# Key pages of a paged stick-breaking decode: one 1024-column product and one segmented sum in place of eight multiply-and-sum instructions

## The chip, the cores and the metric

The kernel runs on one NeuronCore of a Trainium2 chip, in one launch. The metric is the device time of one execution in microseconds (us), and the median of several runs is given. One further execution was taken with the hardware profiler; all rows below are from it.

The engines have these names: PE is TensorE (matrix products; its weight loads are PEld), DVE is VectorE, ACT is ScalarE, POOL is GpSimd, SP is SyncE, which here only issues transfers. They run side by side and wait for each other on semaphores.

## What is computed

The reference is one step of a two-layer decoder over a prompt of 512 rows and 8 sample rows, with width 2048, all in float32. Layer 0 has gated linear attention and retention; layer 1 has stick-breaking attention with 8 heads of 128 and a chunked spatial-gating MLP. Each layer ends in an output projection and a residual. The change lies in layer 1, in the attention of the samples over their past of 2048 positions, held in pages of 128 positions x 8 heads x 128 (512 KB each, 16 pages per sample):

```python
k_past = cache_k[i][page_table].reshape(dec_b, n_past, HC, DC)
z = (jnp.einsum('bqhd,bshd->bhqs', q, k) * (q.shape[-1] ** -0.5)
     + offset.astype(jnp.float32)[None, :, None, None])
log_beta = jax.nn.log_sigmoid(z)
log_rest = jnp.where(mask, jax.nn.log_sigmoid(-z), 0.0)
between = lax.cumsum(log_rest, axis=3, reverse=True) - log_rest
weight = jnp.where(mask, jnp.exp(log_beta + between), 0.0)
```

For a sample there is one query per head, so the scores of a page are 128 x 8 numbers: for each position and head a sum over 128 products of key and query.

## The kernel before

**The products.** All large projections are made in units. A unit is 8 chunks of 128 rows of a weight tile of 128 columns; each weight is split into a high and a low part, and three products (high x high, high x low, low x high) are summed, on two halves of 260 columns: 48 products per unit, all recorded at L548 (the helper `mm`). ACT makes the high part (`hi`, L973, recorded at L971), DVE the low part (`lo`, L1341, recorded at L1349). Both write one of two buffers, so the splits of unit u+2 are made when PE has finished unit u (semaphore `pe_tile`). SP loads the weights into five slots of `raw`.

**The order around the change.** Layer 1 has a first stage `l1a` (16 tiles: queries and the MLP's v) and a second `l1b` with one pass for each of 8 heads, 10 units each. The other work of a stage is written as a Python generator per engine (`l1a_mix`, `mix1`) and is woven between the units by `walk`: after a unit each engine goes one step further in its generator. On DVE `walk` (L1365) first makes the low split of the unit two ahead, and then takes the step. `l1b` runs head 0, then a hardware loop of three bodies with heads 1 and 2, 3 and 4, 5 and 6, then head 7.

**A pass of `l1b`** (`mix1` on DVE, L1818; on PE, L845; on ACT, L1220) does the prompt's attention for head i and the sample attention for sample i, both beside the 10 units. The steps on DVE that matter here:

- step 6 (L1882 to L1885) scales the prompt's scores `z` and takes their absolute value; ACT then runs exp and ln over `za`;
- step 7: `keys(7)`, then L1889 and the masks (L1787) finish `za` ("rest"), which PE's product "between" (L896 to L903) waits for;
- step 8: `keys(8)`, then the argument of a GELU (L1721 to L1723);
- step 9: L1897 on the product's result, `keys(9)`, then masks again ("weight"), which PE's output product (L909 to L915) waits for;
- step 10: L1903 to L1906, then `keys(10)`, the last of the pass.

**The key pages.** `keys(at)` stands at steps 1, 3, 4, 5, 7, 8, 9 and 10 (`KEYS_AT`, L69) and works on two pages of the next sample, i + 1; so head passes 0 to 6 have key pages and pass 7 has none. Sample 0's sixteen pages are worked on in steps 23 to 35 of `l1a` (`KEYS0_AT`, L68), one per step at first, two per step in the last three. `key_page` (L1725) waits for the page's transfer and makes eight `tensor_tensor_reduce` instructions, one per head, each of which multiplies 128 columns of the page by 128 columns of `qb` (the query row, the same on all partitions) in place and sums them into one column of scores. In the trace such an instruction is two records, CUSTOM_DVE_ANT_0 and the read of its accumulator, both at L1733. The last one raises `k_free`.

The pages have five slots: two for keys (`key_slot`, p % 2) and three for values. POOL fetches key pages (`key_page`, L1976, issue at L1982): page p waits for `k_free` of page p - 2. SP fetches value pages (L458) between weight loads, and PE works on them.

**Fences.** DVE instructions that read what the one before wrote are separated by a semaphore: `step(...)` (class `Chain`, L321) lets the instruction raise `dve_step` and waits for it. In a hardware loop the value waited for is worked out from the loop's index and the number of steps per body, which is why `step.body(n, 0, 24)` gets that number.

Of the kernel before, what the change touches and what calls it, by code (L numbers as in the profile page):

```python
# [9 lines left out]
ALU = mybir.AluOpType  # L10
ACT = mybir.ActivationFunctionType

P = 128
# [12 lines left out]
HC = 8  # L26
# [97 lines left out]
def build(nc, a, o, cst):  # L124
    ctx = ExitStack()
    with ctx:
# [5 lines left out]
        def s(name):  # L132
            if name not in sems:
                sems[name] = ctx.enter_context(nc.semaphore(name))
            return sems[name]
# [22 lines left out]
        def region(n):  # L158
            at = used[0]
            used[0] += n  # L160
            assert used[0] <= 16600, used[0]
            return arena[:, at:at + n]
# [50 lines left out]
        pages = region(5 * 1024).rearrange("p (n d) -> p n d", n=5)  # L213
        srow = mrow[:, 128:512]
        brow = mrow
        qb = region(1024)
# [92 lines left out]
        def key_slot(p):  # L309

            return p % 2
# [1025 lines left out]
        def _(dve):  # L1337
            step = Chain(dve, "dve_step")
            tt, ts_, stt, copy = dve.tensor_tensor, dve.tensor_scalar, dve.scalar_tensor_tensor, dve.tensor_copy
# [385 lines left out]
            def key_page(b, p, to):  # L1725

                if p == 0:
                    dve.wait_ge(s("qb"), b * 16 + 16)
                slot = key_slot(p)
                dve.wait_ge(s(f"page{slot}"), b * 128 + 16 * (p // 2 + 1))  # L1730
                for h in range(HC):
                    kpage = pages[:, slot, P * h:P * h + P]
                    last = dve.tensor_tensor_reduce(kpage, kpage, qb[:, P * h:P * h + P], 1.0, 0.0,  # L1733
                                                    ALU.mult, ALU.add, to[:, 8 * p + h:8 * p + h + 1])
                last.then_inc(s("k_free"), 1)

            def key_pages(b, k, to):

                for p in (2 * k, 2 * k + 1):
                    key_page(b, p, to)  # L1740
# [21 lines left out]
            def l1a_mix():  # L1762
                for n in range(L1A_STEPS):
                    for r in range(4):
                        if n == Q_SUM[r] + 1:
                            dve.wait_ge(s("q_rs"), r + 1)
                            for t in range(2):
                                last = stt(wide[:, 2 * r + t, :], G[r % 2 * 2 + t], cols[:, C_QN:C_QN + 1], tmp[t],
                                           ALU.mult, ALU.mult)
                            step(last)  # L1770
                        value_gate(r, n - V_AT[r])
                    if n == Q_SUM[3] + 1:
                        copy(qcol.rearrange("p (b h) -> p h b", b=NB), wide[:, 0:HC, T:N]).then_inc(s("q_col"), 1)
                    for p in range(NPAGE):
                        if n == KEYS0_AT[p]:
                            key_page(0, p, zs[0])
                    yield
# [132 lines left out]
            def l1b(i, odd, last=False):  # L1910
                mix = mix1(i, odd, last)
                walk("l1b", i, L1B_ORDER, None, mix=mix)
                finish(mix)
# [1 line left out]
            l1b(0, 0)  # L1915
            step.straight()
            with dve.Fori(0, 3) as n:
                step.body(n, 0, 24)
                l1b(n * 2 + 1, 1)
                l1b(n * 2 + 2, 0)  # L1920
            step.end(3, 24)
            l1b(7, 1, True)
            rows_kept(8)
            dve.wait_ge(s("pe_tile"), tile_no("out1", 0, 0))
# [229 lines left out]
```

## Time and profile before

| | |
|---|---|
| median of 3 runs | 2234.89 us (2234.24 to 2239.43) |
| the profiled execution | 2237.85 us, its span 2236.3 us |
| mean granted clock of PE | 0.974 of full speed |
| instructions | 45304 |
| PE busy | 2116.0 us (95%) |
| DVE busy | 1156.1 us (52%) |
| ACT busy | 605.5 us (27%) |
| POOL busy | 200.5 us (9%) |
| `l1a` and `l1b`, up to the last output product | about 1140 to 2000 us of the span |

The span is what the program's instructions cover; the time of an execution holds a little more. Busy shares are means over the whole span, so a stage can look quite different. In rows of the chain and the timeline the first number is the start in us from the span's start, the second the length in us; "x16" is the number of instructions that were merged in a row; what stands in brackets is the idle time of the engine before it and what ended it.

### The profile page before, as it was taken

What the parts mean: (1) busy time and instruction counts of PE and PEld (TensorE: products, weight loads), DVE (VectorE), ACT (ScalarE), POOL (GpSimd) and SP (SyncE); (2) the same over time, 40 slices, a digit from 0 to 9 for tenths busy, and PEclk for the clock granted to TensorE, in tenths of its full rate; (3) what the DMA queues carried; (4) which work ended last, traced back from release to release, by engine and by line L of the source; (5) the groups of instructions that cost most, each with busy time, mean ns of one, the idle gap of its engine ahead of it and who ended that gap; (6) DMA issues with size and microseconds to landing.
All of it is one profiled execution on the core that took longest, in us unless ns stands there. A gap on an engine that the chain in (4) does not pass through costs nothing.

```text
span 2236.3 us, 45304 instructions
## 1 busy us (share of the span) xinstructions
PE 2116.0 (95%) x16847; PEld 1868.0 (84%) x16847; DVE 1156.1 (52%) x3617; ACT 605.5 (27%) x773; POOL 200.5 (9%) x319
## 2 busy tenths in 40 slices
PE   6789999999999999899789998999999999999997
PEld 2268888898888888899789996888888888888997
DVE  1543544435445356544452576776677677635332
ACT  1322222222121222322233423233232323324221
POOL 0000101101011011000000011111111111000110
PEclk9989999999999999999899999999999999999999
DMA  9977666566665766343422467798798788763441
GB/s 322 304 229 233 194 185 199 181 209 202 194 206 181 221 185 188 104 116 110 161 84 85 127 208 232 260 298 273 246 300 266 253 287 274 237 181 104 131 134 57
DMA packets 401524, 444.97 MB, mean 199 GB/s; under 512 B 17268, under 2 KB 307406, under 8 KB 399807
## 3 DMA queue, kind: packets, MB, share of 16 engines
q1 hardware_dynamic: 359270, 311.99, 45.4%
q0 software_dynamic: 32288, 122.12, 15.8%
q10 hardware_dynamic: 9810, 8.73, 1.2%
q8 instruction: 103, 1.69, 0.3%
q14 instruction: 53, 0.43, 0.1%
HBM read 416.18 MB, written 26.61 MB: 198 GB/s over the span
## 4 chain that ended last, share of the span: by engine, by line
PE 82%; DVE 9%; ACT 3%; DMA 3%; issue 3%; SPq 0%; DVEq 0%; ACTq 0%; POOLq 0%
PE pt L548 65%; PE m L548 15%; DVE arena L1733 2%; PE m L552 2%; ACT w_hi L971 2%; ACT arena L971 1%; DMA raw<-in_e_w_ada 1%; DVE w_lo L1349 1%; DMA arena<-in_o_k_norm_g 1%; PE pt L552 1%; DVE arena L1897 1%; DVE arena L1787 0%; DMA arena<-in_cache_k 0%; DVE arena L1468 0%; DVE act_lo L1429 0%
## 5 line engine op out<-in xcount | busy, mean ns | idle before, releaser
L548 PE MATMUL pt<-act_hi,w_hi 128*128 128x260 f32 x4384 | 911.9, 290 | 41.7 <-DVE w_lo L1349 13.3
L548 PE MATMUL pt<-act_hi,w_lo 128*128 128x260 f32 x4384 | 891.0, 285 | 0.0
L548 PE MATMUL pt<-act_lo,w_hi 128*128 128x260 f32 x4384 | 889.3, 285 | 0.0
L1349 DVE TENSOR_TENSOR w_lo<-raw,w_hi 128x1024 fp32r<-128x1024 f32 x274 | 335.7, 1225 | 850.3 <-ACT w_hi L971 849.3
L548 PEld LDWEIGHTS pt<-act_hi,w_hi 128*128 128x128 f32 x4384 | 683.7, 191 | 105.3 <-issue 85.4
L548 PEld LDWEIGHTS pt<-act_lo,w_hi 128*128 128x128 f32 x4384 | 684.5, 191 | 0.0
L548 PEld LDWEIGHTS pt<-act_hi,w_lo 128*128 128x128 f32 x4384 | 684.0, 191 | 0.0
L971 ACT ACTIVATE w_hi<-raw 128x1024 fp32r<-128x1024 f32 x274 | 289.9, 1058 | 1156.9 <-PE pt L548 1139.6
L1733 DVE CUSTOM_DVE_ANT_0 arena<-arena 128x128 f32<-128x128 f32 x1024 | 223.9, 287 | 44.6 <-DMA arena<-in_cache_k 44.0
L971 ACT ACTIVATE arena<-arena 128x1040 f32<-128x1040 f32 (+8 forms) x191 | 158.1, 837 | 192.9 <-DVE arena L1833 75.5
L548 PE MATMUL m<-raw,cond 128*9 128x512 f32 x768 | 130.1, 638 | 18.7 <-DMA raw<-in_e_w_ada 16.5
L548 PE MATMUL m<-arena 128*128 128x256 f32 (+6 forms) x704 | 121.7, 383 | 2.3 <-DVE arena L1581 1.5
L1982 POOL DMA_DIRECT2D arena<-in_cache_k x128 | 68.0, 531 | 619.7 <-DVE arena L1733 310.5
L548 PEld LDWEIGHTS m<-arena 128*128 128x128 f32 (+4 forms) x704 | 76.3, 166 | 39.7 <-issue 15.5
L548 PEld LDWEIGHTS m<-raw,cond 128*9 128x9 f32 x768 | 16.6, 90 | 81.5 <-DMA raw<-in_e_w_ada 43.2
L552 PE MATMUL m<-c_ident,arena 128*128 128x128 f32 (+2 forms) x403 | 57.7, 275 | 18.9 <-DMA c_fold<-const_fold 8.9
L2053 POOL TENSOR_SCALAR arena<-arena 128x256 f32<-128x256 f32 x56 | 51.8, 925 | 225.5 <-DVE arena L1574 191.4
L548 PE MATMUL m<-arena,mod 128*8 128x256 f32 x1024 | 67.2, 380 | 0.0
L548 PEld LDWEIGHTS m<-arena,ones 128*128 128x128 f32 (+1 forms) x236 | 41.2, 192 | 31.0 <-issue 15.5
L971 ACT ACTIVATE arena<-m 128x512 f32<-128x512 f32 (+2 forms) x93 | 49.8, 572 | 63.8 <-PE m L548 48.4
L548 PE MATMUL m<-arena,ones 128*128 128x512 f32 (+3 forms) x236 | 60.5, 369 | 5.9 <-DVE arena L1662 5.9
L552 PEld LDWEIGHTS m<-c_ident,arena 128*128 128x128 f32 (+2 forms) x403 | 44.9, 143 | 21.6 <-DMA c_fold<-const_fold 8.9
(169 smaller groups left out, 1135.5 us busy)
## 6 DMA issues: line engine op xcount, KB each, us to landing
arena<-in_cache_k POOLq DMA_DIRECT2D x128, 512.0 KB, 5.0
arena<-in_cache_v SPq DMA_DIRECT2D x128, 512.0 KB, 5.1
raw<-in_o_w_in SPq DMA_DIRECT2D x112, 512.0 KB, 5.7
raw<-in_e_w_in SPq DMA_DIRECT2D x98, 512.0 KB, 4.5
raw<-in_e_w_ada SPq DMA_DIRECT2D x96, 512.0 KB, 5.9
raw<-in_o_w_ada SPq DMA_DIRECT2D x96, 512.0 KB, 5.3
raw<-in_e_w_out SPq DMA_DIRECT2D x32, 512.0 KB, 3.9
raw<-in_o_w_out SPq DMA_DIRECT2D x32, 512.0 KB, 4.7
```

The costliest lines, as they stand in the source:

```text
L548: return pe.matmul(out, lhsT, rhs, start=start, stop=stop, skip_group_check=True)
L552: return pe.transpose(out, x, ident[0:k, 0:k])
L971: return act.activation(out, x, fn, **kw)
L1349: tt(w_lo[:, b, :], raw[:, sl, :], w_hi[:, b, :].bitcast(F32), ALU.subtract)\
L1733: last = dve.tensor_tensor_reduce(kpage, kpage, qb[:, P * h:P * h + P], 1.0, 0.0, ALU.mult, ALU.add, to[:, 8 * p + h:8 * p + h + 1])
L1897: tt(z, z, m012[:, 0:SB_ALL], ALU.subtract).then_inc(s("lw"), 1)
L1982: pool.dma_start(pages[:, key_slot(p), :], ck[bass.ds(page, 1)].rearrange("n s d -> (n s) d"))\
L2053: pool.tensor_scalar(carry[:, n, :], S[:, (n - 1) % 2, :], small[:, 6 * (n // 2) + n % 2:6 * (n // 2) + n % 2 + 1], None, ALU.mult).then_i ...
```

## The change

In `key_page` on DVE the eight instructions become two: one product of the whole page (1024 columns) with the query row, in place, and, behind a fence, one sum over the last dimension of the page seen as 8 heads x 128, which writes all eight score columns. The semaphore `k_free` is raised by the sum. Each page now has one `step`, and a loop body has 32 pages, so the number of steps per body goes from 24 to 56.

```diff
-                for h in range(HC):
-                    kpage = pages[:, slot, P * h:P * h + P]
-                    last = dve.tensor_tensor_reduce(kpage, kpage, qb[:, P * h:P * h + P], 1.0, 0.0,
-                                                    ALU.mult, ALU.add, to[:, 8 * p + h:8 * p + h + 1])
-                last.then_inc(s("k_free"), 1)
+                kpage = pages[:, slot, :]
+                step(tt(kpage, kpage, qb, ALU.mult))
+                dve.tensor_reduce(to[:, HC * p:HC * p + HC], kpage.rearrange("p (h d) -> p h d", h=HC),
+                                  mybir.AxisListType.X, ALU.add).then_inc(s("k_free"), 1)
...
-                step.body(n, 0, 24)
+                step.body(n, 0, 56)
...
-            step.end(3, 24)
+            step.end(3, 56)
```

## Rows read from the trace of the kernel before

**Rows 1.** The page's engine totals: busy us, share of the span, instructions.

```profile
PE 2116.0 (95%) x16847; PEld 1868.0 (84%) x16847; DVE 1156.1 (52%) x3617; ACT 605.5 (27%) x773; POOL 200.5 (9%) x319
```

**Rows 2.** One stretch (the pass of head 1): length, then busy us of PE, PEld, DVE, ACT, POOL.

```profile
1432.00:1516.00 84.00, 83.65 (x699) 72.85 (x698) 60.50 (x314) 25.42 (x34) 9.48 (x18) 1.00 0.84 275
```

**Rows 3.** The chain that ended last, in the pass of head 3.

```profile
1653.45 2.48 DVE arena L1733 x23
...
1659.33 4.60 PE m L548 x20
...
1673.42 2.62 DVE arena L1733 x25
1677.69 5.55 PE m L548 x24
```

**Rows 4.** All that PE waited for from 1516 to 1599 us: in total, times, longest.

```profile
PE pt L548 <- issue: 3.6, 1, 3.6
PE m L548 <- DVE arena L1787: 0.2, 1, 0.2
```

**Rows 5.** DVE's timeline: first instructions of pages 6 and 7, and the low split behind.

```profile
1550.50 0.29 DVE L1733 CUSTOM_DVE_ANT_0 arena<-arena 128x128 f32<-128x128 f32 x1 [1.89 <-DMA arena<-in_cache_k]
...
1552.21 0.28 DVE L1733 CUSTOM_DVE_ANT_0 arena<-arena 128x128 f32<-128x128 f32 x1
...
1554.98 1.23 DVE L1349 TENSOR_TENSOR w_lo<-raw,w_hi 128x1024 fp32r<-128x1024 f32 x1 [1.00 <-ACT w_hi L971]
```

**Rows 6.** DVE's groups by line and shape: busy us, mean ns, idle before.

```profile
L1349 DVE TENSOR_TENSOR w_lo<-raw,w_hi 128x1024 fp32r<-128x1024 f32 x274 | 335.7, 1225 | 850.3 <-ACT w_hi L971 849.3
L1733 DVE CUSTOM_DVE_ANT_0 arena<-arena 128x128 f32<-128x128 f32 x1024 | 223.9, 287 | 44.6 <-DMA arena<-in_cache_k 44.0
L1733 DVE DVE_READ_ACCUMULATOR2_ANT arena<- 128x1 f32 x512 | 42.3, 83 | 0.0
...
L1592 DVE CUSTOM_DVE_ANT_0 arena<-arena 128x256 f32<-128x256 f32 x48 | 17.2, 421 | 4.2 <-ACT arena L971 4.2
...
L1721 DVE TENSOR_SCALAR arena<-arena 128x1040 f32<-128x1040 f32 x4 | 2.8, 702 | 4.6 <-ACT arena L971 4.6
```

**Rows 7.** DVE's timeline in `gate`: L1806, its fence, L1807.

```profile
1528.64 0.69 DVE L1806 TENSOR_TENSOR arena<-arena 128x520 f32<-128x520 f32 x1
1529.36 0.70 DVE L1807 TENSOR_TENSOR arena<-arena 128x520 f32<-128x520 f32 x1
```

**Rows 8.** Timelines of POOL (issues of pages 4 and 6) and DVE (page 4's start).

```profile
1536.80 0.53 POOL L1982 DMA_DIRECT2D arena<-in_cache_k  x1 [8.69 <-DVE mod L1733]
...
1544.04 0.54 POOL L1982 DMA_DIRECT2D arena<-in_cache_k  x1 [5.01 <-DVE mod L1733]
...
1541.53 0.29 DVE L1733 CUSTOM_DVE_ANT_0 arena<-arena 128x128 f32<-128x128 f32 x1 [0.25 <-DMA arena<-in_cache_k]
```

**Rows 9.** Timelines of DVE and ACT between `keys(5)` and the end of the pass.

```profile
1556.39 1.55 DVE L1882 TENSOR_SCALAR arena<-m,per_head 128x1280 f32<-128x1280 f32 x1 [0.18 <-PE m L552]
...
1582.77 1.23 DVE L1349 TENSOR_TENSOR w_lo<-raw,w_hi 128x1024 fp32r<-128x1024 f32 x1 [3.87 <-ACT w_hi L971]
...
1560.43 2.58 ACT L971 ACTIVATE arena<-arena 128x1280 f32<-128x1280 f32 x2 [4.98 <-DVE arena L1884]
1563.19 1.06 ACT L971 ACTIVATE w_hi<-raw 128x1024 fp32r<-128x1024 f32 x1 [0.18 <-PE pt L548]
```

**Rows 10.** The end of `l1a`: a piece of the chain, and PE's wait.

```profile
1324.22 6.96 DMA arena<-in_cache_k
...
PE m L548 <- DVE arena L1842: 8.3, 1, 8.3
```

**Rows 11.** The chain behind a stall of PE, and that stretch (PE, PEclk, DMA, GB/s).

```profile
1598.85 7.36 PE pt L548 x48
1606.55 5.87 PE pt L548 x48
...
1596.00:1600.00 4.00, 1.15 (x5) 0.50 1.14 332
```

## The prediction

> **What bounds the kernel now.** I read the page's engine totals first, then the stretches of layer 1, then the chain of waits, then what PE itself waits for. The totals say that PE is busy for 95% of the span and DVE for 52% [rows 1]. A reader may stop there and call DVE's work free. The change touches only the key pages, and these are worked on in the sample attention, once per head pass of `l1b` and for sample 0 at the end of `l1a`; so I read that stretch alone. In one pass of 84 us PE is busy for 83.65 us and DVE for 60.50 us [rows 2]. There DVE still has 23 us to spare on average.
>
> The chain of waits shows where the average misleads. In a pass it leaves PE twice, each time through key pages [rows 3]: `keys(7)` (pages 8 and 9) stands ahead of `za` and its masks, which the second triangular product of PE ("between") needs, and `keys(9)` (pages 12 and 13) stands ahead of the masks of `weight`, which the output product needs. Both times a PE unit and the chain `pe_tile`, high split, low split, keys, masks have come out equally long: PE's whole wait there is 0.2 us [rows 4]. So the PE is the bound, but with no slack behind these two blocks. Whatever they grow by, PE waits.
>
> **The cost of a page.** Before: eight multiply-and-sum instructions. Two pages run from 1550.50 to the 1.00 us idle that ends at 1554.98, and the second page begins 1.71 us after the first [rows 5]. One instruction lasts 287 ns, and its accumulator read 83 ns, but they overlap: eight in 1.71 us is 0.213 each [rows 5, 6]. Take 1.70 us a page.
>
> After: a `tensor_tensor` of 1024 fp32 columns. This form is in the trace, with two SBUF inputs of the same size: 1225 ns [rows 6]. Then the fence. The multiply is now waited for before the sum may read it. A fenced pair in the gate starts 0.72 us apart with a first instruction of 0.69 us [rows 7], so the fence costs 0.03 us after the end and the overlap of about 0.08 us is lost. Then a `tensor_reduce` of 1024 columns to eight sums, which no row shows. From below, a one-input operation over 1040 columns takes 702 ns; from above, a two-input one over 1024 takes 1225 ns [rows 6], and a separate start for each of the eight segments would add 8 x 0.08 = 0.64 us to that. I take the upper row, because the two summing forms that the trace has, 128 columns in 287 ns and 256 in 421 ns [rows 6], go at 1.05 ns a column, and 287 + 896 x 1.05 gives 1.23 us. What follows starts 0.08 us before its end. A page is then 1.23 + 0.03 + 1.23 - 0.08 = 2.40 us, 0.70 us more than before. With the lower row it is 1.88 us (+0.18), with a start for each segment 3.0 us (+1.3).
>
> The Trainium skill ("VectorE: DVE Perf Modes", The perf-mode tier table) gives `tensor_reduce` only the one-element rate, by which the sum would stay as it is and the second rival below would have no place; no row here shows it.
>
> Nothing else is moved. The step counts per loop (24 to 56) only keep the fence's arithmetic right. DMAs, their queues and POOL's order are as before, but a page's slot is given back 0.70 us after a later start, and this matters below.
>
> **The blocks one by one, in a steady pass** (three of the eight key blocks cost time directly or through pages; each block is two pages, so +1.4 us).
>
> `keys(9)`: the chain from `pe_tile` to the output product grows by 1.4 us, PE waits 1.4 us. `keys(7)`: the same, 1.4 us.
>
> `keys(1)`, `keys(3)`, `keys(4)`, `keys(5)` lie beside PE units, which have their splits two units ahead, so their own length is hidden by that lead. But they are tied together by the pages: there are two slots, so page p+2 is asked for only when page p is done, and lands 4.7 to 6.5 us later. Page 4 is issued at 1536.80 and DVE already waits for it at 1541.53; page 6 is issued at 1544.04, and DVE waits 1.89 us for it, until 1550.50 [rows 5, 8]. So the delay adds up: page 2 comes free 3 x 0.70 = 2.1 us later, page 4 starts 2.1 later and is free 2.8 later, page 6 starts 2.8 later, and page 7 ends 4.2 us later. The pass also begins late by 0.7, because pages 14 and 15 close the one before, behind the same kind of wait: 4.9 us. Against this stand three pieces of cover: the 1.00 us wait ahead of the low split at 1554.98, and 0.18 us each ahead of the scores' scaling (L1882) and of ACT's next high split [rows 5, 9]. The other five passes are taken to be like this one. What is left, 4.9 - 1.36 = 3.5 us, goes through ACT: its two passes over `za` end at 1563.01 and the high split stands right behind them [rows 9], then the low split, then `keys(7)`. So PE waits 3.5 + 1.4 = 4.9 us before "between".
>
> `keys(8)` is covered: DVE waits 3.87 us for the high split behind it [rows 9]. `keys(10)` leaves the 0.7 us at the pass's end that is counted above.
>
> A steady pass is 3.5 + 1.4 + 1.4 = 6.3 us longer. Key pages are worked on in seven passes (the last head has none). The first of them begins behind the 8.3 us stall of `l1a` [rows 10] with its pages landed, so I leave the chain of pages out of it: 2.8 us. Six others: 38 us.
>
> **The clock.** PE's only stall of such a size inside these passes is 3.6 us at a loop's back edge; the clock granted over it is 0.50 and the 48 records after it take 7.36 us in place of 5.87 us [rows 4, 11]. The new 4.9 us stall is longer, so I expect the granted level to fall from 2.4 to 1.2 GHz for a while: 1.4 to 1.5 us (7.36 - 5.87) for each of six, 8.5 us. The 1.4 us stalls are too short by the rows that I have.
>
> **Sample 0, in `l1a`.** Here PE waits already: 8.3 us for the sample's softmax chain behind page 15 [rows 10]. The chain runs from page to page: page 13 is asked for at 1324.22, when page 11 is done, and lands 6.96 us later, while DVE and PE wait [rows 10]. On this path lie pages 4, 9, 11, 13, 14 and 15, so 6 x 0.70 = 4.2 us.
>
> Sum: 38 + 2.8 + 8.5 + 4.2 = 53.5 us. The profiled execution took 2237.85 us (span 2236.3) and would go to 2291.4; it lies 3 us above the median of the three runs, 2234.89, against which I forecast 2288.4 us, 2.4% slower. A measurement can tell about 0.3% (6.7 us) from no change.
>
> **Rivals.**
>
> *Not slower.* If the price of a DVE instruction is its full duration, eight of 287 ns and eight accumulator reads of 83 ns are 2.96 us [rows 6], and two of 1.23 us are 2.46: 0.5 us less. It decides at a page of 1.70 us. But PE would gain almost nothing: 0.2 us twice in a pass, seven times, and 6 x 0.5 = 3 us in `l1a`, so about 2229 us. Against it: eight start in 1.71 us [rows 5]. The Trainium skill states this rule ("VectorE: DVE Perf Modes", The DRAIN you can't avoid, and Rules for kernel authors): an instruction waits until the pipe is empty, so count operations and not semaphores. The trace disagrees, 213 ns apart at 287 ns of length. Chance 0.04.
>
> *The reduction at two columns a cycle.* Page +0.18 us; the page chain is then inside its cover (7 x 0.18 = 1.2 us against 1.36), and 4 x 0.18 us in seven passes plus 1.1 us give +6 us: 2241. For it: one-input forms do reach it [rows 6]. Against: the summing forms don't. Chance 0.08.
>
> *Pages don't add up.* If the transfers, now further apart, land faster, or ACT has room, only `keys(7)`, `keys(9)` and `l1a` count: 7 x 2.8 + 4.2 = 24 us and no clock loss, 2259 us. For it: landings vary between 4.7 and 6.5 us [rows 8]. Chance 0.18.
>
> *Each segment pays a start.* Page +1.3 us: 7 x 1.3 - 1.36 + 4 x 1.3 = 12.9 us a pass, six times, plus 8.5, some 9 for the first pass and 8 for `l1a`: +103 us, 2338. Chance 0.08.
>
> **How the numbers follow.** The forecast has 0.62, with 2270 to 2310 as its own range (a page at +0.6 to +0.8 moves it by 10 x 0.1 x 6 = 6 us, the clock by 8). The range reaches down to the third rival and half of what lies between, 2252, and up to 2316; the first, second and fourth rivals, 0.20 together, lie outside. Faster 0.02; the first rival's rest and most of the second, 0.08, within 0.3%; slower 0.90.
>
> **What would show it.** In the profile after: L1732's multiply at 1.22 us, the sum at 1.15 to 1.23 us, 2.40 us from page to page; DVE busy some 70 us in a pass; PE waits of 4 to 5 us before "between" and 1.4 us before the output product, put down to L1787; a granted clock below 1 after the first; page waits on `in_cache_k` about as long as now; passes of 90 us in place of 83. I am wrong if PE's waits on L1787 stay under a microsecond, or if `keys(7)` starts where it did relative to its PE unit.

## The result, and the profile after

| | before | after |
|---|---|---|
| median, of runs taken side by side | 2235.68 us (4 runs) | 2296.26 us (4 runs, 2287.61 to 2304.53) |
| ratio, 95% interval | | 1.0267 [1.0239, 1.0295] |
| profiled execution (span) | 2237.85 us (2236.3) | 2287.61 us (2286.1) |
| mean granted clock of PE | 0.974 | 0.967 |

The change makes the kernel 60.6 us, 2.7%, slower. 2288.4 us was forecast, and the median lies in the range given (2252 to 2316). The profiled execution is the fastest of the four, 8.7 us under the median, so the rows below account for 50 us and not for 60.6. One execution of a kernel below, e9, took 7080 us, and it counts in no ratio.

The engine totals, to be laid beside [rows 1]: PE does the same number of instructions and its share falls by two points; DVE has half the instructions and is busy for 79 us more.

```profile
PE 2125.5 (93%) x16847; PEld 1875.9 (82%) x16847; DVE 1235.3 (54%) x1825; ACT 605.0 (26%) x773; POOL 199.7 (9%) x319
```

DVE's groups by shape, the page's two instructions (compare [rows 6]). 1219 ns for the product, 1220 ns for the sum:

```profile
L1732 DVE TENSOR_TENSOR arena<-arena 128x1024 f32<-128x1024 f32 x128 | 156.1, 1219 | 60.3 <-DMA arena<-in_cache_k 59.9
L1733 DVE TENSOR_REDUCE arena<-arena 128x8 f32<-128x1024 f32 x64 | 78.1, 1220 | 2.2
```

Three passes (heads 1, 2 and 3; length, then busy us of PE, PEld, DVE, ACT, POOL, then PEclk), for [rows 2]. A pass was 84 us with PE busy for all but 0.35 us of it; now these stretches are 90 to 98 us, and PE is idle for 6.7 to 8.4 us of it (head 2's stretch ends with the 3.6 us of a loop's back edge, and head 3's begins with the slow unit behind it):

```profile
1432.00:1524.00 92.00, 85.34 (x688) 73.71 (x688) 70.54 (x91) 26.31 (x34) 10.04 (x19) 0.96 0.78 251
1524.00:1614.00 90.00, 82.25 (x680) 71.41 (x680) 70.00 (x91) 26.33 (x34) 10.04 (x19) 0.97 0.81 264
1614.00:1712.00 98.00, 89.58 (x715) 77.76 (x715) 70.26 (x91) 26.23 (x34) 10.03 (x19) 0.95 0.72 236
```

What PE waits for on the masks that "between" and the output product need, from 1430 us to the end of the passes (total, times, longest), in the kernel before and then after:

```profile
PE m L548 <- DVE arena L1787: 1.5, 6, 0.2
```

```profile
PE m L548 <- DVE arena L1786: 39.9, 12, 6.9
```

What DVE waits for there on key pages, before and after:

```profile
DVE arena L1733 <- DMA arena<-in_cache_k: 34.0, 26, 2.9
```

```profile
DVE arena L1732 <- DMA arena<-in_cache_k: 54.9, 31, 4.1
```

DVE's timeline in the pass of head 2: pages 2 and 3, then the starts of pages 5 and 7, and POOL's issues of these two:

```profile
1545.79 1.22 DVE L1732 TENSOR_TENSOR arena<-arena 128x1024 f32<-128x1024 f32 x1
1547.04 1.22 DVE L1733 TENSOR_REDUCE mod<-arena 128x8 f32<-128x1024 f32 x1
1548.18 1.22 DVE L1732 TENSOR_TENSOR arena<-arena 128x1024 f32<-128x1024 f32 x1
...
1550.57 1.22 DVE L1349 TENSOR_TENSOR w_lo<-raw,w_hi 128x1024 fp32r<-128x1024 f32 x1
...
1556.75 1.23 DVE L1732 TENSOR_TENSOR arena<-arena 128x1024 f32<-128x1024 f32 x1 [1.29 <-DMA arena<-in_cache_k]
...
1565.33 1.22 DVE L1732 TENSOR_TENSOR arena<-arena 128x1024 f32<-128x1024 f32 x1 [1.89 <-DMA arena<-in_cache_k]
```

```profile
1551.37 0.53 POOL L1981 DMA_DIRECT2D arena<-in_cache_k  x1 [1.86 <-DVE mod L1733]
...
1559.95 0.53 POOL L1981 DMA_DIRECT2D arena<-in_cache_k  x1 [3.23 <-DVE mod L1733]
```

Product to sum is 1.25 us (the fence), sum to the next product 1.14 us (no fence), a page 2.39 us. Page 4 had just landed, 4.0 us after its issue at 1548.98; pages 5 and 7 start 5.4 us after their issue, and DVE stands for them. In the chain of waits of the next pass these two transfers are pieces of their own, which they were not before, and PE's 20 products of "between" take 6.84 us where [rows 3] has 4.60:

```profile
1644.32 6.72 DMA arena<-in_cache_k
...
1654.26 7.43 DMA arena<-in_cache_k
...
1681.23 6.84 PE m L548 x20
```

PE's stalls pass by pass, worked out from the starts and ends of its instructions, with the length of the 20 products behind the first of them and DVE's waits for pages 4 to 7 (us):

```
head                          0     1     2     3     4     5     6
stall before "between"     1.67  5.18  2.67  6.94  6.24  5.20  4.80
the 20 products behind it  4.60  6.08  4.60  6.84  6.43  6.05  6.19
waits for pages 4 and 6     1.1   0.0   0.1   0.0   2.7   0.5   0.0
waits for pages 5 and 7     0.0   6.1   3.2   6.9   2.7   5.1   5.1
stall before the output    1.53  1.48  1.47  1.47  1.47  1.48  1.48
```

### The profile page after: what moved, and what is told of

Its sections match the earlier page's. It is cut to its first block, busy times and chain, and to the rows that moved or that the text cites. A ratio compares the mean times of both kernels' runs of the same rounds, so it can differ in the third digit from the quotient of the medians.

```text
span 2286.1 us, 43608 instructions
## 1 busy us (share of the span) xinstructions
PE 2125.5 (93%) x16847; PEld 1875.9 (82%) x16847; DVE 1235.3 (54%) x1825; ACT 605.0 (26%) x773; POOL 199.7 (9%) x319
## 4 chain that ended last, share of the span: by engine, by line
PE 67%; DVE 14%; DMA 7%; issue 6%; ACT 4%; DVEq 0%; ACTq 0%; SPq 0%; POOLq 0%
PE pt L548 54%; PE m L548 12%; DMA arena<-in_cache_k 4%; DVE arena L1732 4%; ACT arena L971 2%; ACT w_hi L971 2%; DVE w_lo L1349 2%; DMA raw<-in_e_w_ada 1%; PE m L552 1%; DVE arena L1733 1%; DMA arena<-in_o_k_norm_g 1%; DVE arena L1786 1%; DVE mod L1733 1%; PE pt L552 1%; DVE arena L1896 1%
## 5 line engine op out<-in xcount | busy, mean ns | idle before, releaser
L971 ACT ACTIVATE arena<-arena 128x1040 f32<-128x1040 f32 (+8 forms) x191 | 158.1, 837 | 240.8 <-DVE arena L1832 89.8
L1732 DVE TENSOR_TENSOR arena<-arena 128x1024 f32<-128x1024 f32 x128 | 156.1, 1219 | 60.3 <-DMA arena<-in_cache_k 59.9
L548 PE MATMUL m<-raw,cond 128*9 128x512 f32 x768 | 128.2, 633 | 18.0 <-DMA raw<-in_e_w_ada 15.8
L1733 DVE TENSOR_REDUCE arena<-arena 128x8 f32<-128x1024 f32 x64 | 78.1, 1220 | 2.2
L1733 DVE TENSOR_REDUCE mod<-arena 128x8 f32<-128x1024 f32 x64 | 78.1, 1220 | 2.2
L548 PE MATMUL m<-arena,c_from_key 128*128 128x128 f32 (+3 forms) x80 | 31.7, 481 | 41.6 <-DVE arena L1786 32.7
```

The lines of the kernel that those rows point to most:

```text
L548: return pe.matmul(out, lhsT, rhs, start=start, stop=stop, skip_group_check=True)
L971: return act.activation(out, x, fn, **kw)
L1732: step(tt(kpage, kpage, qb, ALU.mult))
L1733: dve.tensor_reduce(to[:, HC * p:HC * p + HC], kpage.rearrange("p (h d) -> p h d", h=HC), mybir.AxisListType.X, ALU.add).then_inc(s("k_fre ...
```

## The experiments

Line numbers in rows of an experiment are its own, so the masks are L1786, L1793 or the like. All ratios are to the kernel before, run side by side on the same chip. Differences between experiments of different groups are differences of such times, so some us of them can be the chips'.

**The new page in one place at a time.** Four kernels take the new form for some pages and keep the old eight instructions for the others. Each has this edit (here e1, for `keys(7)` and `keys(9)`), with its own condition and step count:

```diff
+                if p in (8, 9, 12, 13) and not (isinstance(b, int) and b == 0):
+                    kpage = pages[:, slot, :]
+                    step(tt(kpage, kpage, qb, ALU.mult))
+                    dve.tensor_reduce(to[:, HC * p:HC * p + HC], kpage.rearrange("p (h d) -> p h d", h=HC),
+                                      mybir.AxisListType.X, ALU.add).then_inc(s("k_free"), 1)
+                else:
+                    for h in range(HC):
...
-                step.body(n, 0, 24)
+                step.body(n, 0, 32)
```

In e2 the condition is `p < 8` (blocks 1, 3, 4 and 5 of the passes, count 40), in e4 `p in (10, 11, 14, 15)` (blocks 8 and 10, count 32), both without sample 0; in e3 it is sample 0 alone.

> Only the blocks keys(7) and keys(9) of a pass have the product and the segmented sum; all other pages are worked on as before. Theory (a block is 1.4 us longer, and these two blocks stand on the path that PE waits on): PE waits 1.5 to 1.7 us before 'between' and 1.5 us before the output product in each of seven passes, no loss of clock, and the time is 2235 + 7 x 2.8 = 2255 us (range 2250 to 2260). Rival (the loss comes from the sum of delays over all pages or from DVE's load as a whole, not from the place): four of sixteen pages changed give a quarter of the 53 to 60 us, some 2249 us, and PE waits well under 1 us in each place.

Measured: 2253.73 us, ratio 1.0085 [1.0061, 1.0108]. What PE waited for in the passes of heads 1 to 6:

```profile
PE m L548 <- DVE arena L1793: 18.5, 12, 1.6
```

Twelve waits, none over 1.6 us: 1.61 before "between" and 1.48 before the output product in every pass. Here the two blocks cost what two longer pages cost (2 x 0.70 = 1.4 us, on the 0.2 us that PE waited before "between" already [rows 4]), and there is no variation between passes.

> Only keys(1), keys(3), keys(4) and keys(5) (pages 0 to 7) of samples 1 to 7 have the new form. None of these blocks stands on the path from a unit's end to a product of PE. Theory (delays add up through the two page slots, 6 x 0.70 = 4.2 us at the end of page 7, of which 1.4 us are covered): PE waits 2.5 to 3.5 us before 'between' in passes 1 to 6 and under 0.3 us before the output product; the time is 6 x 2.8 = 17 us longer, 2252 us, up to 2260 if stalls of 3 us also cost clock. Rival (only a block's own place on PE's path counts): no wait over 0.3 us and a time within 4 us of before.

Measured: 2268.18 us, 1.0134 [1.0115, 1.0153]. It costs more than e1, though none of these pages stands on PE's path by its place in the order:

```profile
PE m L548 <- DVE arena L1793: 26.6, 6, 5.7
```

Six waits, all before "between": 5.25, 3.79, 5.07, 5.67, 3.95 and 2.88 us, a mean of 4.4. The direction is that of the theory, the size is over what it gave, and it varies from pass to pass as after the change and unlike e1. That points to the transfers; the pair e7 and e8 below tests it for the whole change.

> Only sample 0's sixteen pages, in l1a, have the new form. Theory: the chain of pages 4, 9, 11, 13, 14, 15 gets 6 x 0.70 = 4.2 us longer, and PE's waits in l1a sum to some 18 us in place of 14: 2239 us (2237 to 2241). Rival: sample 0's pages are hidden by the weights' transfers and the long softmax chain, no change.

Measured: 2238.29 us, 1.0003 [0.9990, 1.0017], so at most 3.8 us and perhaps nothing. Its profile has the three stalls of `l1a` at 4.47, 4.34 and 8.75 us against 3.79, 2.32 and 8.29 before, 3.2 us more. The trace of one execution shows the stalls, the times do not show a cost; I count this one as open.

> Only keys(8) and keys(10) (pages 10, 11, 14, 15) of samples 1 to 7 have the new form. Theory: keys(8) is covered by DVE's wait of 3.9 us behind it; keys(10) ends 0.7 us later, and the next pass's 1.4 us of cover takes that up, so no PE wait is over 0.5 us and the time is that of before within 4 us (2233 to 2239). Rival (every page costs its 0.7 us somewhere): 28 pages x 0.7 = 20 us, 2255.

Measured: 2237.54 us, 1.0009 [0.9999, 1.0019]: no cost that shows. The four ratios add up to +0.0231, some 52 us, against +0.0267 for the whole change; what is left is about as large as the intervals.

**Without the transfers.** In e7 and e8 the key pages are not fetched at all; DVE works on the query row in their place and waits for its own count alone, and of POOL's waits for free slots one per sample is left, the one ahead of the query row's transfer. The samples' scores are left out of the computation by this. e7 is the kernel before, e8 the kernel after (there the page's wait goes in the same way).

```diff
-                dve.wait_ge(s(f"page{slot}"), b * 128 + 16 * (p // 2 + 1))
+                if not (isinstance(b, int) and b == 0 and p < 2):
+                    dve.wait_ge(s("k_free"), b * 16 + p - 1)
...
-                    last = dve.tensor_tensor_reduce(kpage, kpage, qb[:, P * h:P * h + P], 1.0, 0.0,
+                    last = dve.tensor_tensor_reduce(kpage, qb[:, P * h:P * h + P], qb[:, P * h:P * h + P], 1.0, 0.0,
...
-                page = pool.value_load(ptab[0:1, bass.ds(b * NPAGE + p, 1)], min_val=0, max_val=NPOOL - 1)
-                if p >= 2 or not first:
-                    pool.wait_ge(s("k_free"), b * 16 + (p - 1))
+                if p == 1 and not first:
+                    pool.wait_ge(s("k_free"), b * 16)
                     pool.sem_inc(s("pool_waited"), 1)
-                pool.dma_start(pages[:, key_slot(p), :], ck[bass.ds(page, 1)].rearrange("n s d -> (n s) d"))\
-                    .then_inc(s(f"page{key_slot(p)}"), 16)
```

> The kernel before, without its 128 key page transfers: the eight instructions of a page multiply the query row by itself into the page's slot, with the same sizes, and nothing waits for a page (sample scores are left out, so samples' outputs differ). It is the base for the run that follows. Theory: PE's two 0.2 us waits per pass stay, l1a's stalls shrink by what its pages' transfers held up (2 to 7 us): 2228 to 2234 us.

> The changed kernel without its key page transfers, in the same way. Theory (a part of the stall before 'between', some 3.6 of 5.2 us, is made of page transfers asked for later, and only 1.4 us is the block's own length): PE waits 1.6 us before 'between' and 1.5 us before the output product in each of seven passes, no clock is lost, and it is 20 us (0.9%) slower than the run before it, not 60. Rival (the 5 us come from DVE's longer total work in keys(1) to keys(7), whatever the transfers do): the stalls of 4 to 6 us stay and it is 45 us or more slower than the run before it.

Measured: e7 2229.59 us, 0.9968 [0.9956, 0.9980]; e8 2257.31 us, 1.0089 [1.0068, 1.0109]. PE's waits in the passes of heads 1 to 6 of e8 are those of e1 again:

```profile
PE m L548 <- DVE arena L1787: 18.6, 12, 1.6
```

So the longer page by itself costs 2257.31 - 2229.59 = 27.7 us, where 20 were expected. The change cost 60.6, and the rest needs the transfers: (2296.26 - 2257.31) - (2236.63 - 2229.59) = 32 us. That is more than half, from a resource that the change doesn't touch, and it is close to what the prediction gave for the chain of pages and the clock, 6 x 3.5 + 8.5 = 29.5 us. The transfers as such did not get slower: in the passes of heads 1 to 6 a page landed 5.2 us after its issue before the change and 5.1 us after it, in the mean. In `l1a`, e8 has waits of 5.8 and 11.2 us where e7 has 3.8 and 7.7, which is 5.5 us on top of the 20 in the passes. One more thing falls out: e8's four runs lie within 0.6 us of each other (2257.00 to 2257.61) and e7's seven within 2.3, those of the kernel after within 17 us and the four of the kernel before beside them within 5. Most of the spread comes with the transfers too.

**The blocks moved behind the masks.** e5 is the kernel after and e6 the kernel before with `keys(7)` and `keys(9)` behind the masks that PE waits for, not ahead of them:

```diff
-                keys(7)
                 dve.wait_ge(s("z_l"), i + 1)
                 step(stt(za, z, 0.0, za, ALU.max, ALU.add))
                 masks(za).then_inc(s("rest"), 1)
+                keys(7)
...
-                keys(9)
                 dve.wait_ge(s("w_e"), i + 1)
                 masks(za).then_inc(s("weight"), 1)
+                keys(9)
```

> The changed kernel with keys(7) moved behind the masks of 'rest' and keys(9) behind the masks of 'weight' in their steps; all work as in the changed kernel. Theory: the block keys(7), 4.8 us in place of 3.4 us, leaves PE's path; the wait before 'between' falls from 5.2 to about 0.5 us and that before the output product from 1.5 to under 1 us, since nothing but the 3.5 us of page delay is left against 3.4 us gained. But pages 8, 9, 12 and 13 are given back 2 to 5 us later, so pages 14 and 15 come later, and part of it may turn up as a new wait of PE for a low split at the start of a pass (up to 3 us). 2245 to 2262 us, most of the 60 us back. Rival (DVE's total work in a pass is the limit, wherever it stands): the same waits come back in other places and the time stays over 2280 us.

> The kernel before with the same two moves. Theory: PE waited only 0.2 us in these places, fourteen times, so 1 to 3 us at most are to be had, 2232 to 2236 us, and the interval holds no change. Rival: the blocks held up more than the waits show (the low splits behind them), 5 us or more faster.

Measured: e5 2289.27 us, 1.0221 [1.0194, 1.0248]; e6 2245.41 us, 1.0035 [1.0025, 1.0044]. My theory failed in both: e5 was to be near 2250 us and gains 7 us on the kernel after (by the ratios 0.5%, with intervals that touch), and e6 is 8 us slower than the kernel before. What PE waits for in e5's passes:

```profile
PE m L548 <- DVE arena L1786: 15.8, 10, 2.6
PE m L548 <- DVE arena L1792: 12.6, 4, 4.3
```

and what DVE waits for there:

```profile
DVE arena L1732 <- DMA arena<-in_cache_k: 70.4, 31, 4.3
```

The kernel after has 54.9 us there, 31 times. PE's waits on masks fell from 39.9 to 15.8 us, but the pages are given back later and are waited for longer, and 12.6 us of PE's wait reappear at L1792, a copy in step 1 of the next pass. In e6 it is this, against 34.0 us, 26 times in the kernel before:

```profile
DVE arena L1733 <- DMA arena<-in_cache_k: 84.4, 43, 4.6
```

The order of the work had been hiding the transfers: two pages worked on early are two pages asked for early. e5's passes take 91.5 to 95.7 us, no less than those of the kernel after (89.8 to 96.4). Its rival gave the time, over 2280 us, but not by its cause: e8 has the same work of DVE in a pass, and its passes take 85.7 to 91.8 us. Nor is the chain of transfers a bound of its own that runs through the whole pass. From the end of one page to the end of the next one in its slot it takes 0.72 us until POOL starts the issue (page 3's sum ends at 1550.65, page 5 is issued at 1551.37), about 5.4 us until page 5 is worked on and 2.4 us for it: 8.5 us, eight times in a pass 68 us, under PE's 83. And 61 of the 96 pages of e5's heads 1 to 6 had landed more than 0.1 us before DVE took them. I read e5 as DVE's waits for some pages standing between its work for PE, but no run tests this, and how much a better order of the steps could win back stays open.

**Is it the fence, or the product's length, or the sum's?** In e11 the sum takes only the first 2 of the 128 products of each head (the rest of each score is left out); everything else is the kernel after.

```diff
-                dve.tensor_reduce(to[:, HC * p:HC * p + HC], kpage.rearrange("p (h d) -> p h d", h=HC),
+                dve.tensor_reduce(to[:, HC * p:HC * p + HC], kpage.rearrange("p (h d) -> p h d", h=HC)[:, :, 0:2],
```

> The changed kernel, with the sum over only the first 2 of each head's 128 products (the other 126 are left out of the samples' scores): the sum shrinks from 1.22 to some 0.16 us, a page to about 1.4 us, which is 0.3 us less than before the change, with the same fence, the same transfers and the same semaphores. Theory (only the length of a page matters, and below 1.70 us PE has nothing to gain but its 0.2 us waits): all 60 us come back and no more than 5 us beyond, 2229 to 2236 us, no PE wait over 0.3 us in a pass. Rival (the fence, or the whole-page product with its later release of POOL, costs something of its own): it stays 10 us or more above before.

Measured: 2229.34 us, 0.9964 [0.9953, 0.9975]. DVE's timeline:

```profile
1520.69 1.23 DVE L1732 TENSOR_TENSOR arena<-arena 128x1024 f32<-128x1024 f32 x1
1521.95 0.17 DVE L1733 TENSOR_REDUCE mod<-arena 128x8 f32<-128x16 f32 x1
1522.03 1.22 DVE L1732 TENSOR_TENSOR arena<-arena 128x1024 f32<-128x1024 f32 x1
```

A page is 1.34 us, and PE has no wait on the masks. One product of 1024 columns in place of eight of 128, and the fence, cost nothing beyond their share of the page's length: with the sum short the loss is gone. A page of this length is 8 us faster than before. Its trace lacks the 1.5 us of waits on masks and two half-rate stretches of the clock that the trace of before has (named below); the rest of the 8 us isn't traced to a place. The same timeline gives the price of the fence: 1.26 us from product to sum, for an instruction of 1.23.

**Both products first.** e12 makes the products of a block's two pages, then the two sums, with one fence for the pair.

```diff
-                    key_page(b, p, to)
...
+                    kpage = pages[:, key_slot(p), :]
+                    last = tt(kpage, kpage, qb, ALU.mult)
+                    if p % 2 == 0:
+                        last.then_inc(s("dve_step"), 1)
+                        step.n += 1
+                    else:
+                        step(last)
+                for p in (2 * k, 2 * k + 1):
+                    kpage = pages[:, key_slot(p), :]
+                    dve.tensor_reduce(to[:, HC * p:HC * p + HC], kpage.rearrange("p (h d) -> p h d", h=HC),
+                                      mybir.AxisListType.X, ALU.add).then_inc(s("k_free"), 1)
```

> The changed kernel, with a block's two products first and its two sums behind, so that the fence is covered: a block 4.6 in place of 4.8 us, but the first page is given back 1.1 us later and a block can't work on its first page's sum while the second page is still on its way. Theory (pages' return and landing carry most of the stall): where the second page is waited for (pages 5, 7 and 15) the overlap is lost, 1.1 us each, against 0.2 us won in each block: 5 to 20 us slower than the changed kernel, 2300 to 2316 us. Rival (DVE's busy time decides): 7 to 10 us faster than it, 2286 us.

Measured: 2322.51 us, 1.0387 [1.0363, 1.0410], 26 us slower than the kernel after. DVE's work is slightly shorter (two products 2.35 us, two sums 2.35 us), but the even page is given back 1.2 us later, behind the odd page's product, and the odd page's transfer must have landed before the even page can be finished:

```profile
1567.55 1.22 DVE L1743 TENSOR_TENSOR arena<-arena 128x1024 f32<-128x1024 f32 x1 [1.77 <-DMA arena<-in_cache_k]
1571.38 1.23 DVE L1743 TENSOR_TENSOR arena<-arena 128x1024 f32<-128x1024 f32 x1 [2.61 <-DMA arena<-in_cache_k]
1572.64 2.35 DVE L1751 TENSOR_REDUCE mod<-arena 128x8 f32<-128x1024 f32 x2
```

PE's stalls before "between" are 7.30, 6.49, 8.14, 6.93, 7.92 and 7.42 us, a mean of 7.4 against 5.2. The direction was expected, the loss is larger. The instructions are the same, only their order and one fence differ, so the loss is that of the later return and of the wait for both pages; this run doesn't tell these two apart.

**A better place for sample 0's pages.** The kernel before has 14.4 us of stalls of PE beside sample 0's pages (3.79, 2.32 and 8.29), the kernel after 17.9. e9 and e13 are the kernel before with the pages spread otherwise over its units:

```diff
-KEYS0_AT = [23, 24, 25, 26, 27, 28, 29, 30, 31, 32, 33, 33, 34, 34, 35, 35]
+KEYS0_AT = [23, 23, 24, 25, 25, 26, 27, 27, 28, 29, 29, 30, 31, 31, 32, 33]
```

That is e9; in e13 the list is 23, 23, 24, 25, 26, 28, 28, 29, 29, 30, 30, 31, 32, 33, 33, 34.

> The kernel before, with sample 0's pages of l1a earlier: one or two per step from step 23 on, the last at step 33, where before six pages stood in the last three steps. Theory (the last pages' transfers, asked for one after the other with DVE waiting, are what PE waits for at the end of l1a): PE's 2.3 us wait for a low split goes and the 8.3 us wait shrinks, 4 to 8 us faster, 2227 to 2232 us. Rival (the 8.3 us are ACT's and DVE's softmax and gate chain, whatever the pages do): within 2 us of before.

> The kernel before, with the key pages of sample 0 spread over the units of l1a once more, so that none is placed at unit 27, ahead of the low split there. The version before this one (KEYS0_AT 23 23 24 25 25 26 27 27 ...) ended at 2231.4 us, with a stall of PE of 7.6 us at the unit after two pages and 3.4 us at a later one. Theory: PE stalls in l1a because a page stands ahead of a split that PE wants, so without a page at unit 27 the 7.6 us stall goes or falls under 3 us, and the end of l1a has 3 to 5 us left: 2226 to 2229 us. Rival: the sixteen pages come no faster than two transfers at a time let them, so the stall only moves to the units behind and the time stays within 1 us of 2231.4.

Measured: e9 2231.42 us, 0.9976 [0.9962, 0.9990]; e13 2229.96 us, 0.9975 [0.9962, 0.9988]. What PE waited for in `l1a`, in e9:

```profile
PE pt L548 <- DVE w_lo L1349: 7.6, 1, 7.6
PE m L548 <- DVE arena L1842: 3.4, 1, 3.4
```

and in e13:

```profile
PE m L548 <- DVE arena L1842: 6.3, 1, 6.3
PE pt L548 <- DVE w_lo L1349: 3.1, 2, 1.9
PE pt L548 <- ACT w_hi L971: 2.3, 1, 2.3
```

e9 is in its range, though not as I thought: the 8.3 us shrank to 3.4, but the two stalls ahead of it, 3.79 and 2.32, became one of 7.6. In e13 that one did go, as I expected, and its time came back elsewhere: 11.7 us of stalls in the rows above against 11.0 in e9. The rival was right about that, and e13 missed its range of 2226 to 2229 us. Both arrangements beat the kernel before by a quarter of a per cent, some 6 us, and are not told apart.

## Why the prediction was right, step by step

**The page.** 2.40 us was forecast from 1.23 + 0.03 + 1.23 - 0.08; 2.39 was measured, each term within 0.01 to 0.02 us. The choice that mattered was the sum's length between 0.70 and 1.87 us, and going by the rows of the summing forms was right: 1220 ns. The Trainium skill ("VectorE: DVE Perf Modes", The perf-mode tier table) has `tensor_reduce` at the one-element rate, and the trace of after agrees: 1024 columns take as long as in the two-input product, while L1721's 1040 took 702 [rows 6]. That removes the rival of two columns a cycle, and the rival of a start for each segment too. The first rival, that a DVE instruction costs its full duration, falls with e1: two blocks with it are 1.4 us longer, not shorter.

**`keys(7)` and `keys(9)`.** 1.4 us of PE wait each was forecast. Before the output product it is 1.47 to 1.53 in every pass; before "between" e1 and e8 show 1.6 alone. Right.

**What costs nothing.** `keys(8)` and `keys(10)`: e4 finds no cost. Right for `keys(8)`; the 0.7 us counted for the end of the pass is too small to be seen.

**The chain of pages.** 3.5 us was forecast, on top of the 1.4, so 4.9 in all; the mean of the six steady passes is 5.17, of which 0.24 stood there before. The size came out and the working did not. I had the delay run through the even pages because DVE waited for pages 4 and 6 in the pass that I read [rows 5, 8], and I took the time from issue to landing as it was. After the change it is the odd ones that are late. Page 4 landed 4.7 to 5.4 us after its issue before the change and 3.6 to 5.1 us after it; page 5 went from 4.6 to 5.0 us to 5.4 to 6.7, and page 7 from 4.8 to 6.2 us to 5.4 to 7.4. So DVE's waits for pages grew from 34.0 to 54.9 us, where I had written that they would stay about as long. Counted from the start of page 0, page 7 ends 3.7 to 7.4 us later than before, 5.5 in the mean, where the count of pages gives 4.2. By the odd pages that count is the same (four pages up to the end of page 3, then 5, then 7), so that the wrong path gave the right sum is luck. PE's stall follows these waits in the table above: 3.3 us of waits and 2.67 of stall for head 2, 6.9 and 6.94 for head 3. So "the other five passes are taken to be like this one" was the weak step. They are not alike: 2.67 to 6.94 us. That 32 us of the loss go with the transfers in e8 shows that the chain of pages is real, and "pages don't add up" falls. Why the odd page's transfer takes longer and the even one's shorter than before is not shown.

**The clock.** 8.5 us was forecast, from [rows 11]. The 20 products behind the stall took 4.60 us in the two passes with the shorter stalls (1.67 and 2.67 us), and 6.05 to 6.84 in the five with 4.80 us or more. The granted clock behind the 2.67 us stall, behind the 6.94 us one, and in the first part of the latter:

```profile
1584.80:1589.40 4.60, 4.56 (x21) 1.00 0.94 351
1681.20:1688.00 6.80, 6.77 (x21) 0.66 0.50 184
1681.20:1684.00 2.80, 2.77 (x4) 0.50 1.03 394
```

0.66 is a mean over a stretch that begins at half the full rate, 1.2 GHz in place of 2.4. Together the five lose 1.48 + 2.24 + 1.83 + 1.45 + 1.59 = 8.6 us. Right in the sum, though on five of the six passes, at 1.7 us each instead of 1.4: two errors that cancel. Not in it are short stretches at 0.50 behind the output product, three after the change (from 1522.0, 1897.5 and 1989.6 us, some 3 us each) and two before it (from 1683.9 and 1939.9 us, with no stall over 0.24 us ahead of them in their passes); one more of them costs some 1.7 us, an estimate from half its length, and what brings them is not shown.

**Sample 0.** 4.2 us was forecast. The traces have 3.9 (the span from the first stall to the end of the last is 65.2 us before and 69.2 after), e8 against e7 has 5.5, but e3's time shows nothing, with at most 3.8 us in its interval. The term is at best right and may be too large.

**The sum.** 53.5 us against 60.6, with an interval of 53.4 to 66. In the two traces it is 49.8, of which the six steady passes (from one L1888 to the next) make 46.4, where 38 + 8.5 was forecast: stalls of PE grew by some 38 us, and the clock took most of the rest. The trace of after is also 4.4 us ahead when DVE starts sample 0's first page (1258.12 in place of 1262.48), where nothing was changed; from there on the loss is 54.2 us. The other three runs are 6 to 17 us slower than this one. The term that may be short is the chain of pages, since the time of the same kernel moves that much from run to run, and little without the transfers. The size of that term in the three slower runs is not known, since only the fastest has a trace.

## What to carry to other kernels

Where several instructions become two, ask what the new ones do per element: here each element is passed over twice, 2 x 1.22 us a page, while the eight with the sum in them took 1.70. An engine at 54% busy sets the time if what it gives back (a buffer, a mask) is late. And when work is moved to take it off a path, look at what it releases: moved behind the masks, the key pages cost the kernel before 8 us, because the next transfer is asked for at their end, and DVE waited 84 us for pages in place of 34.

## What the runs showed of the chip that was not expected

- A semaphore between two DVE instructions is not free: 1.25 us from start to start with it, 1.14 without, for instructions of 1.22 us. The Trainium skill ("VectorE: DVE Perf Modes", The DRAIN you can't avoid) has the chain with a semaphore after each take as long as the one without; in this trace the difference is 0.11 us.
- A sum of eight segments of 2 elements takes 0.17 us and one of eight segments of 128 takes 1.22: a new segment has no price that shows.
- From issue to landing a 512 KB page takes 3.6 us at best and 7.9 at worst in the passes of heads 1 to 6 after the change (3.6 to 7.5 before it), with two slots and the weights' transfers beside it. The four runs of the kernel after differ by 17 us; without these transfers four differ by 0.6 (e8) and seven by 2.3 (e7).
